# One of two unread products taken out of each attention head step of a hybrid decoder trunk

## The reference

```python
for layer in range(DEPTH):                       # DEPTH = 2
    i = layer // 2
    if layer % 2 == 0:
        h = h + attn_mixer(rmsnorm(h, attn_norm[i]), ...)   # 8 windowed heads + 8 latent heads
    else:
        h = h + gla_mixer(rmsnorm(h, gla_norm[i]), ...)     # chunked gated linear attention
    h = h + peer_ffn(rmsnorm(h, ffn_norm[layer]), ...)      # 8 x 16 experts of 16384, gathered per token
return rmsnorm(h, final_norm)[:, N_META:]
```

## Time and profile before

| what | value |
|---|---|
| median of 3 runs | 1893.31 us |
| lowest, highest run | 1893.27, 1904.49 us |
| profiled execution, its own time | 1906.0 us |
| its span, first to last instruction | 1904.2 us |
| mean granted TensorE clock of it | 0.918 of full |

### The profile page before, as it was taken

One profiled execution on the slowest core, in us unless ns is written; L12 is line 12 of the kernel. 1 busy time (PEld: TensorE's weight loads), 2 busy tenths in 40 slices (PEclk: granted clock), 3 DMA queues, 4 the chain that ended last, 5 costly groups with the idle time before them and its releaser, 6 DMA issues.

```text
span 1904.2 us, 14545 instructions
## 1 busy us (share of the span) xinstructions
PE 1487.1 (78%) x4063; PEld 675.9 (35%) x4063; DVE 1110.6 (58%) x2719; ACT 357.7 (19%) x910; POOL 1052.6 (55%) x1111
## 2 busy tenths in 40 slices
PE   8999977498887774799988874988888738767776
PEld 3466544145322221344433522433334313222222
DVE  3344255686555555765786656666876556645552
ACT  1033202112221111121221111221211211111110
POOL 1111033666666666556676565766665657656664
PEclk9999997798999987899989997999999979998999
DMA  5112046999998888799999997999999889988897
GB/s 180 63 72 74 15 168 237 418 345 350 370 384 353 352 342 348 294 362 392 417 418 418 370 381 301 396 418 417 418 418 399 319 331 356 384 338 347 346 383 260
DMA packets 184126, 616.74 MB, mean 324 GB/s; under 512 B 19275, under 2 KB 20811, under 8 KB 184054
## 3 DMA queue, kind: packets, MB, share of 16 engines
q0 software_dynamic: 152064, 553.72, 74.5%
q1 hardware_dynamic: 31990, 62.17, 8.7%
HBM read 614.77 MB, written 1.05 MB: 323 GB/s over the span
## 4 chain that ended last, share of the span: by engine, by line
PE 30%; DVE 19%; DMA 15%; issue 14%; POOL 13%; another core or an unknown queue 8%; ACT 0%; DVEq 0%; SPq 0%; POOLq 0%
POOL arena L607 13%; PE bank L892 11%; DMA arena<-peer_u,idx 9%; PE bank L685 8%; DVE arena L1602 8%; DMA arena<-peer_v,idx 5%; PE bank L866 2%; PE bank L787 2%; PE bank L793 2%; DMA wring<-gla_w_in 1%; PE bank L748 1%; PE bank L759 1%; DVE best L1549 1%; PE bank L841 1%
## 5 line engine op out<-in xcount | busy, mean ns | idle before, releaser
L892 PE MATMUL bank<-arena 128*128 128x512 f32 x1920 | 953.7, 636 | 339.6 <-DMA arena<-peer_v,idx 164.5
L1602 DVE CUSTOM_DVE_ANT_0 arena<-arena,bank 128x1024 f32<-128x1024 f32 x528 | 625.3, 1217 | 274.2 <-DMA arena<-peer_u,idx 188.1
L607 POOL DMA_INDIRECT arena<-peer_u,idx x528 | 511.7, 969 | 337.9 <-issue 140.0
L892 PEld LDWEIGHTS bank<-arena 128*128 128x128 f32 x1920 | 359.9, 199 | 892.3 <-issue 454.6
L607 POOL DMA_INDIRECT arena<-peer_v,idx x528 | 511.2, 968 | 281.6 <-issue 149.7
L685 PE MATMUL bank<-wring,hT 128*128 128x512 f32 (+5 forms) x604 | 262.2, 589 | 5.0 <-issue 2.8
L1197 ACT ACTIVATE arena<-con,wgt 128x128 f32<-128x128 f32 x480 | 153.3, 390 | 356.3 <-issue 170.6
L685 PEld LDWEIGHTS bank<-wring,hT 128*128 128x128 f32 (+1 forms) x604 | 108.8, 182 | 151.7 <-issue 145.1
L1186 ACT ACTIVATE gl<-dots 128x16 f32<-128x16 f32 x33 | 7.1, 216 | 401.3 <-issue 228.8
L572 POOL TENSOR_TENSOR small<-small,con 128x1 f32<-128x1 f32 (+2 forms) x12 | 8.1, 677 | 120.3 <-DVEq L1368 71.1
L1611 DVE SCALAR_TENSOR_TENSOR h<-arena,wgt,h 128x1024 f32<-128x1024 f32 x48 | 61.6, 1284 | 20.7 <-DMA arena<-peer_v,idx 20.7
(11 more groups left out here) (157 smaller groups left out, 1011.3 us busy)
## 6 DMA issues: line engine op xcount, KB each, us to landing
wring<-gla_w_in SPq DMA_DIRECT2D x12, 2048.0 KB
arena<-peer_u,idx POOLq DMA_INDIRECT x528
arena<-peer_v,idx POOLq DMA_INDIRECT x528
wring<-gla_w_out SPq DMA_DIRECT2D x4, 2048.0 KB
wring<-peer_w_query SPq DMA_DIRECT2D x4, 2048.0 KB
wring<-attn_w_in SPq DMA_DIRECT2D x2, 2048.0 KB
wring<-attn_w_out SPq DMA_DIRECT2D x2, 2048.0 KB
gws<-peer_w_query SPq DMA_DIRECT2D x2, 2048.0 KB, 10.3
```

What stands on the lines that cost most here:

```text
L607: nc.gpsimd.indirect_dma_start(out=ring[:, slot, :], out_offset=None, in_=table.rearrange("l e d -> (l e) d"), in_offset=bass.IndirectOffs ...
L892: last = nc.tensor.matmul(yacc[:, 512 * i:512 * i + 512], wdiag[:, k, :], vrow[:, v_slot(g, k), 512 * i:512 * i + 512], start=first, stop= ...
L1602: v.tensor_tensor_reduce(out=rows, in0=rows, in1=xnow, scale=1.0, scalar=0.0, op0=ALU.mult, op1=ALU.add, accum_out=dots[:, g % 2, k:k + 1] ...
```

## The change

The second `keep_warm()` of a head step, the one ahead of the transposes of probabilities, is taken out. The function itself and the first call stay, and nothing else differs.

```diff
                 if -1 in live:
                     head_values(i - 1)
                 if 0 in live:
-                    keep_warm()
                     transpose_probs(i, par)
 
             pe.wait_ge(heads_ready, 1)
```

## The result

The kernel after takes 1872.77 us (median of 4 executions, 1868.85 to 1878.22) against 1893.64 us before (median of 4, 1893.27 to 1904.49). The ratio is 0.9878, with a 95% interval of 0.9835 to 0.9921. The profiled execution took 1873.27 us.

The account below looks back on a forecast made before the run. TensorE bounds the heads, whose time counts in full ahead of DMA-busy gathers. Saving 14.5 us for products, less 0.2 for a late copy and 2.0 for the clock, gives 12.3: 1893.3 - 12.3 = 1881.0 us, range 1875 to 1893.

Parts of the forecast that it names:

- The bound: Inside the heads the chain is TensorE's program alone, one step taking 6.25 us with no other engine in it.
- The products: In the heads, 16 of 32 unread products go, all on the path: 15 x 0.91 + 0.86 = 14.5 us saved.
- The covers: ScalarE's later copy is covered by 1.8 us in the loop; in step 14 the values lose some 0.2 us once.
- The clock: TensorE's clock stays full in the loop and falls one piece earlier behind the last scores: 2 us lost.
- my bound (values, transposes and values at half speed): Upper bound of the clock loss at the end of the heads: 1.94 + 0.66 + 1.94 = 4.5 us more.
- The loop stays at full clock, with little to spare: In the heads' loop, one product per 5.34 us step still holds TensorE's clock; no loss was counted.
- The shift to the end: Behind the heads, everything to the first gather and the gathers themselves move forward by the full saving.
- with a little for the spread of the runs: 1875: Low end of the range: full 14.5 us plus 3 us from a shorter slow stretch gives 1875.8, rounded down to 1875.
- the heads' steps are so regular that I carry the difference over unchanged: The 12.3 us gain, worked out on an execution 12.7 us above the median, is subtracted from the median 1893.3.
- runs of the same kernel differ by 11.2 us, as much as the gain: Support for the rival that the gathers absorb the gain, giving 1892; it and another no-gain rival have 0.15 together.
- The slower one: Rival: clock falls in steps 2 to 12, 4.6 us more per slow step, 1916 if half are slow; chance 0.10.
- the thinned piece: Values and two sets of transposes in a loop step, 3.56 us without a long product, where the clock might fall.

Follow-up runs that it names:

- Experiment 7: Kernel before with a third unread product in each head step, next to the second: 1749.39 us in one execution.
- experiment 1: The changed kernel run once more, unaltered: median 1878.40 us of 12 executions, ratio 0.9966 to the kernel before.
- experiment 9: The changed kernel run a third time, unaltered, on a chip with little spread: 1726.79 us, ratio 0.9944 to the kernel before.
- experiment 3: Changed kernel plus 14 unread products in a row behind the heads, spending the saved time again: mean 1903.3 us, ratio 1.0121 to the kernel before.
- experiment 8: Changed kernel plus some 450 small products of zeros ahead of rows mixed in the gathers: 1729.39 us, ratio 0.9963 to the kernel before.
- quiet sets: Second and third sets of executions, on other chips than the first; kernel before mean 1735.5 and 1735.6 us, standard deviation 2.6 and 2.3.
- experiment 10: Changed kernel plus 14 unread products behind the heads, repeated where the spread is small: 1736.05 us, ratio 1.0000 to the kernel before.
- experiment 11: Kernel before with the second product kept only in steps 13 to 15, repeated where the spread is small: 1724.81 us, ratio 0.9937.
- experiment 12: Changed kernel plus two unread products in the wait ahead of the heads and one behind the transposes of steps 14 and 15: 1718.89 us, ratio 0.9903.
- experiment 5: Changed kernel with the first unread product of a head step taken out too, so none left: 1757.26 us, ratio 1.0127 to the kernel before.
- experiment 6: Kernel before without the product ahead of the scores, keeping the one ahead of the transposes of probabilities: 1735.72 us, ratio 0.9996.
- first set: The first four follow-up runs with the kernel before beside them; its 29 executions had mean 1895.6 us, standard deviation 12.3, from 1868.4 to 1911.1.
- experiment 2: Changed kernel plus eight small unread products at the front, restoring the instruction count behind the heads: mean 1882.7 us, ratio 1.0015 to the kernel before.
- experiment 4: Kernel before with the second product kept only in steps 13 to 15: mean 1878.6 us, ratio 0.9964 to the kernel before.

## Why the prediction was wrong, point by point

**The bound (right in the loop).** TensorE alone is the chain there, as before. At the last steps it is not: from 183.94 to 187.29 the chain runs through the mask and exponentials of head 15 and ScalarE's copy. At step 0 TensorE now waits 0.20 us for the exponentials, where before it had the product to do. I had said that the start is not touched.

**The products (right).** I took 15 x 0.91 + 0.86. From the transposes of head 0 to the product ahead of the scores of head 15 there are 13 steps; before they took 196.53 - 114.54 = 81.99 us and after 182.13 - 111.73 = 70.40, which is 11.6 less, 0.89 a step. Experiment 7 adds one and pays 0.87. That is near the 0.91 that I took for each of the fifteen.

**The covers (right).** ScalarE's copy is late by its wait for the exponentials and nobody in the loop waits for it. At the end it is ScalarE's copy that releases the values, at 187.29, as forecast: the wait is 0.81 us in place of 0.68, so 0.13 lost where I took 0.2.

**The clock (right in kind, its terms partly mis-sized).** The fall came not one piece earlier but three, ahead of the values of head 14, with 3.4 us for each of the last two groups of values: it is my bound (values, transposes and values at half speed) and not its middle, though it costs less than the 4.5 that I gave it. From the product ahead of the scores of head 15 to the output transposes it took 12.62 us before and 14.40 after, with two products of 0.91 less: a loss of 3.6, the 0.13 included. The output projection and what follows gave 1.1 back (50.07 to 48.97), which I had named as a possibility. Net it is 2.5, where I had 2.0 and 0.2. What I had not counted: the start of the heads changes from execution to execution. Without the product the first steps took 7.48 us (104.25 to 111.73) in place of 9.63, 1.3 less than the product alone would give, because the clock came back earlier; experiments 1 and 9 had it come back at about 112 to 113, and experiments 3, 7 and 8 never lost it before the loop. That 1.3 and the 0.66 by which the heads began earlier belong to this execution and not to the change; without them the 13.7 would be 11.8. "The loop stays at full clock, with little to spare" was nearly right: of ten traces whose loop has the one product, six show a single slow stretch in it (among them all five of the quiet sets) and four none. It is worth 1.5 to 1.7 us in the 13 steps, where I had priced one at 3.4.

**The shift to the end (right).** Experiments 9, 10, 11 and 12 took 1476.3, 1476.5, 1477.7 and 1476.3 us from the first gather to the end, with the first gather at 248.75, 257.55, 246.92 and 242.07.

**The step that failed** is the last one, "with a little for the spread of the runs: 1875", and, in the sum, "the heads' steps are so regular that I carry the difference over unchanged". The 12.7 us by which the profiled execution lay above its median are no property of the kernel: after the change the profiled execution lies 0.5 us above its median. The spread sits behind the heads: of the 20.9 us, 13.7 are at the first gather of the one execution that was profiled, and the remaining 7.2 lie behind it. Three executions of 1893.3 and one of 1904.5 made it look like a value and an outlier; 29 executions show one broad distribution with a standard deviation of 12.3 us, and 12 of the change one of 14.3. The difference of two means of four then has a standard error of about 9 us (the root of 12.3²/4 + 14.3²/4 is 9.4). 20.9 measured against an effect of 10 to 13 is an ordinary draw, and that it fell outside the range is chance; that it is chance follows from the spread and from experiments 9 and 10, and the eight executions themselves cannot show it. I had even written this down as a rival ("runs of the same kernel differ by 11.2 us, as much as the gain"), but let it raise only the high end. It works both ways: eight times in ten is 1.3 such errors, some 12 us, on either side of 1881.0: 1869 to 1893. The forecast gain itself, 12.3, lies within the interval of the ratio in the quiet set (0.9926 to 0.9961, which is 6.8 to 12.8 us), but more than two standard errors above the 9.7 of the means, and within one of 15.9. So it was a little high; the slow stretch in the loop (1.5 us) and the loss at the last steps (3.6) are what the traces show on that side.

**The rivals.** The slower one, a fall of the clock in the loop, touches the change in one step at most, and befalls its neighbours in full: with none of the products (5) it is all but total, with the other one left (6) it takes the whole gain. The price that I gave for a step at the low clock, 9.98 us with a product, was a little high: without one it is 7.98, and the values take 3.32 where I had 3.80.

The Trainium skill, in "TensorE: Matmul & The Clock Gate", Part 4, says that the full clock does not engage for transposes. The slow loop that I drew from this for the change did not come: its step of 5.35 us has 1.66 us of transposes, and four traces of ten stay at 1.00 through the whole loop. I had called the thinned piece "nearly empty" by that rule, but 1.90 of its 3.56 us are values, which are products. Whether transposes count was not tested by itself. The 16 transposes at 1.00 last only 2.00 us, behind long products, and are weak evidence.

**What stays open.** Why the gathers moved 369 to 380 GB/s with a spread of 12 us in one set and 410 to 413 with 2.3 to 2.6 in the others is not settled. The stretch of 300 to 1700 us in experiment 9:

```profile
300.00:1700.00 1400.00, 1160.56 (x2936) 493.39 (x2935) 986.07 (x2316) 292.70 (x705) 998.81 (x1029) 0.97 1.02 413
```

The kernel is the same as that of experiment 1, so the cause is outside of it; which (the chip, its memory, other cores) no run here can tell. In the first set the time goes with TensorE's time at the low clock (0.27 to 0.51 us for each us; 0.20 or less in the quiet sets), but what leads and what follows was not separated there. Nor is it settled that the gain is the same where the gathers are slow: the three kernels of the first set with shorter heads (experiments 1, 2 and 4) lie 15.3 us below the kernel before in the mean, with a standard error of 2.9, and the first gathers account for 10.7 to 13.4 of it. What held the clock through the loop, and what brought it back in experiment 5, is open too.

## What to carry to other kernels

A product that nobody reads is paid for by its start-to-start time wherever TensorE is the chain; it earns that only where the clock would fall without it. Try it in more than one place: here the same 16 products less gave 10 us when those left stood next to the scores and nothing when they stood among values and transposes, and four placed in waits gave 7 us more. And before a difference under 1% is read from four executions, look at which stage spreads them: read the effect at the end of its own stage (here the first gather), and give the range the spread on both sides.

## What the runs showed of the hardware

- TensorE without a gap stayed at 0.50 for 83 us (112 to 195, experiment 5) with transposes, scores and values of 64 columns, and with the same pieces ran at 1.00 from 202 to 208. A busy TensorE in the profile does not tell its clock.
- Of two places for the same product, the one next to the scores left at most one short fall of the clock in the loop (ten traces), the one between values and transposes eight (experiment 6, one trace). At the low clock such a product takes 1.71 us, and the six products of values 3.36 in place of 1.90.
- The same program has its clock fall and come back at different places in different executions: the first gather was at 245.50, 248.49 and 248.75 in three of them.
- The same kernel took 1895.6 us in the mean on one chip and 1735.5 and 1735.6 on two others, and the difference lies from the first gather to the end (1615 to 1649 against 1474 to 1480 us in the profiled executions of all kernels).
